# Another timetable for the last four adding transfers of a fourth weight block, in both layers of a two-layer trunk

## What is computed

```python
def squared_relu_mlp(u, w_up, w_down):
    return jnp.square(jax.nn.relu(u @ w_up)) @ w_down      # w_down: 4096 x 1024

def reference(x, mem, ...):
    ...
        h = h + rmsnorm(mixed, norm_mix_post[i])
        f = squared_relu_mlp(rmsnorm(h, norm_mlp_pre[i]), w_up[i], w_down[i])
        h = h + rmsnorm(f, norm_mlp_post[i])
```

## Time and profile before

| what | value |
|---|---|
| median of 3 runs | 1269.98 us (1269.67 to 1271.86) |
| the profiled execution | 1271.68 us |
| its span in the trace | 1269.9 us |
| TensorE busy | 1258.7 us, 99% |
| VectorE, ScalarE, GpSimd busy | 926.9, 754.0, 162.0 us |
| granted TensorE clock | 0.999 |
| HBM read and written | 225.69 and 70.04 MB |

### The profile page before, as it was taken

How to read it: one execution, slowest core, us unless ns; L and a number is a source line. 1 busy time by engine, 2 the same in 40 slices (tenths; PEclk the granted TensorE clock), 3 DMA queues, 4 the chain that set the end, 5 groups by cost and what they waited for, 6 DMA issues and landing times.

```text
span 1269.9 us, 19583 instructions
## 1 busy us (share of the span) xinstructions
PE 1258.7 (99%) x7655; PEld 1087.2 (86%) x7655; DVE 926.9 (73%) x1264; ACT 754.0 (59%) x1277; POOL 162.0 (13%) x195
## 2 busy tenths in 40 slices
PE   9999999999999999999999999999999999999998
PEld 7787878888888989999788898778889999988886
DVE  5676775989753786687797974877567776868887
ACT  6655355678653655567565753777564566665663
POOL 0046355363000000000000000000000000000000
PEclk9999999999999999999999999999999999999999
DMA  8488876352585357949876527656227378679854
GB/s 278 146 274 268 240 170 172 109 169 86 145 220 133 121 211 214 225 150 220 251 249 190 194 76 168 131 122 150 83 67 237 132 180 231 195 202 274 245 179 149
DMA packets 110387, 230.29 MB, mean 181 GB/s; under 512 B 8135, under 2 KB 18647, under 8 KB 110039
## 3 DMA queue, kind: packets, MB, share of 16 engines
q1 hardware_dynamic: 84240, 159.93, 38.1%
q0 software_dynamic: 21760, 67.11, 24.2%
q10 hardware_dynamic: 4294, 2.00, 0.8%
HBM read 225.69 MB, written 70.04 MB: 233 GB/s over the span
## 4 chain that ended last, share of the span: by engine, by line
PE 93%; DVE 2%; DMA 2%; ACT 2%; issue 1%; SPq 0%; DVEq 0%; ACTq 0%
PE G L2380 33%; PE G L2876 4%; PE G L2878 4%; PE G L2880 4%; PE X L2839 4%; PE X L2837 4%; PE X L2835 4%; PE X L2403 4%; PE X L2876 3%; PE X L2878 3%; PE X L2880 3%; PE X L2465 3%; PE G L2465 3%; PE G L2839 3%; PE G L2837 3%; PE G L2835 3%
## 5 line engine op out<-in xcount | busy, mean ns | idle before, releaser
L1380 ACT ACTIVATE whi<-raw 128x1024 fp32r<-128x1024 f32 x112 | 118.1, 1058 | 108.6 <-DMA raw<-tsum 31.1
L2132 DVE TENSOR_TENSOR wlo<-raw,whi 128x1024 fp32r<-128x1024 f32 x112 | 135.1, 1220 | 50.0 <-ACT whi L1380 49.6
L1580 DVE TENSOR_TENSOR wlo<-raw,whi 128x1024 fp32r<-128x1024 f32 x77 | 94.6, 1229 | 79.8 <-ACT whi L868 79.8
L1298 ACT ACTIVATE whi<-raw 128x1024 fp32r<-128x1024 f32 x84 | 88.8, 1060 | 103.1 <-PE X L2839 52.6
L2065 DVE TENSOR_TENSOR wlo<-raw,whi 128x1024 fp32r<-128x1024 f32 x84 | 102.7, 1222 | 58.2 <-ACT whi L1298 57.6
L2380 PE MATMUL G<-uhi,whi 128*128 128x512 f32 x352 | 144.8, 411 | 0.2 <-DVE ulo L1597 0.2
L2380 PE MATMUL G<-uhi,wlo 128*128 128x512 f32 x352 | 137.7, 391 | 0.0
L2380 PE MATMUL G<-ulo,whi 128*128 128x512 f32 x352 | 137.3, 390 | 0.0
L868 ACT ACTIVATE whi<-raw 128x1024 fp32r<-128x1024 f32 x77 | 81.4, 1058 | 77.1 <-PE G L2380 29.9
L770 POOL DMA_DIRECT2D tsum<-in_w_down x32 | 32.9, 1040 | 622.0 <-PE G L2380 328.0
L2876 PE MATMUL G<-whi,left_hi 128*128 128x512 f32 x224 | 87.4, 390 | 0.7 <-DVE wlo L2132 0.7
(11 more groups left out here) (457 smaller groups left out, 3691.2 us busy)
## 6 DMA issues: line engine op xcount, KB each, us to landing
tsum<-in_w_down POOLq DMA_DIRECT2D x48, 1024.0 KB, 10.1
raw<-in_w_up SPq DMA_DIRECT2D x64, 512.0 KB, 5.9
raw<-tsum SPq DMA_DIRECT2D x64, 512.0 KB, 4.1
raw<-in_w_down SPq DMA_DIRECT2D x48, 512.0 KB, 5.1
raw<-in_ssd_w_out SPq DMA_DIRECT2D x16, 512.0 KB, 4.3
raw<-in_swa_w_in SPq DMA_DIRECT2D x16, 512.0 KB, 4.4
csrow<-cs_rows SPq DMA_DIRECT2D x16, 384.0 KB, 4.5
raw<-in_swa_w_out SPq DMA_DIRECT2D x12, 512.0 KB, 3.9
```

Source lines behind the costliest of these rows:

```text
L1298: act.activation(whi[n % 4][:, :, :], up_right(g, r, q), ACT.Copy).then_inc(hi_done, up_fill(g, k))
L1380: act.activation(whi[n % 4][:, :, :], down_raw[n % 4][:, :, :], ACT.Copy).then_inc(hi_done, 1)
L1580: dve.tensor_tensor(wlo[q][:, :, :], src[:, :, :], whi[q][:, :, :].bitcast(F32), ALU.subtract).then_inc(lo_done, 1)
L2132: dve.tensor_tensor(wlo[n % 4][:, :, :], down_raw[n % 4][:, :, :], whi[n % 4][:, :, :].bitcast(F32), ALU.subtract).then_inc(lo_done, 1)
```

## The change

Only the two tuples are changed. Every transfer is still issued, in the same order, by the same engine. Of layer 0 the last four numbers were 117, 121, 124, 128 and become 126, 133, 150, 157, that is panels -3, 1, 4, 8 of the down phase become 6, 13, 30, 37. Of layer 1 they were 262, 268, 274, 280 and become 259, 267, 282, 289, that is panels 6, 12, 18, 24 become 3, 11, 26, 33. So the four transfers of a layer lie within 31 panels of its down phase, two ahead of the load of scale rows (panel 16) and two behind it.

```diff
 COPY_AT = (2, 4, 6)
-W0_SUM_AT = tuple(range(54, 64, 2)) + (72, 74) + tuple(range(77, 121, 4)) + (121, 124, 128)
-W1_SUM_AT = tuple(range(182, 196, 2)) + (208, 210) + tuple(range(213, 257, 4)) + (262, 268, 274, 280)
+W0_SUM_AT = tuple(range(54, 64, 2)) + (72, 74) + tuple(range(77, 117, 4)) + (126, 133, 150, 157)
+W1_SUM_AT = tuple(range(182, 196, 2)) + (208, 210) + tuple(range(213, 257, 4)) + (259, 267, 282, 289)
```

## The result

Side by side on the chip (22 runs each) the changed kernel takes 1273.06 us at the median and the kernel before 1271.13 us; the ratio is 1.0016, with a 95% interval of 1.0009 to 1.0022. So it is 2.0 us (1.1 to 2.8) slower. The forecast was no change, 1269.9 us with a range up to 1272.4; the measured time lies outside, 3.2 us above the forecast. Two things came together. The kernel before itself is 1.15 us slower here than the three runs that were shown (1269.98), and the sum had the wrong sign. One run of 2520.42 us, among the 11 of e5, is left out of its ratio; what made it so long is not known.

A forecast was written before the change was run, and what follows sets the result against it. TensorE was taken as the bound, busy 1258.7 of 1269.9 us, with 1.2 us to win. The terms -1.2 + 0.9 + 0.2 = -0.1 us gave 1269.9 us, range 1268.5 to 1272.4.

The forecast's parts named there:

- 1.2 us is all that a new timetable can win: Down phases: TensorE lost 1.2 us at panels 13 and 14 of layer 0, none in layer 1; 0.1% of the time.
- Removed, -1.2: Layer 0, panels 13 and 14: waits blamed on two overlapping adding transfers go away, -1.2 us.
- Panel 13's transfer, +0.9: Layer 0: the transfer moved to panel 13 delays panel 20's held-back load behind two scale rows; a stall of 0.9 us.
- Layer 1, panel 3, +0.2: Layer 1: the transfer moved to panel 3 delays panel 9's load; a stall between 0 and 1.2 us, taken as 0.2.
- The others cost nothing: Transfers at layer 0's panels 30 and 37 and layer 1's 11, 26 and 33 cause no stall, 0 us.
- One adding transfer in the steady part is covered: Steady down phase: a load may take 14.4 us before TensorE waits; beside an adding transfer it takes up to 12.4 us.
- s(n): Start of down-phase panel n, counted at 2.72 us a panel; the panel must have landed 2.3 us before it.
- signs of being right: No wait at layer 0's panels 13 and 14, about a microsecond at panel 20, none or little at layer 1's panel 9.
- one of being wrong: Signs against: a wait still at layer 0's panel 12 or 13, any in panels 30 to 48, or panel 20 in time.
- The slower rival: Held-back load meets the transfer: 3.1 us stall at layer 0's panel 20, 1.2 at layer 1's panel 9; 1273.1 us, chance 0.10.
- faster: Whole kernel: a gain that measurement can tell from no change, about 0.2% or 2.5 us; chance 0.03.
- M6 becomes the wait: Layer 0's last transfer holds back M6's first load by 1.7 us, with 9 us to spare; still 1269.9 us, chance 0.03.

The follow-up runs named there:

- e5: Kernel before, with both layers' four transfers at panels 10, 23, 28 and 33 of the down phase; ratio 0.9988 to the kernel before, median 1270.09 us.
- e8: The changed kernel again with no edit, for a second profile; layer 0's down phase 155.96 us, layer 1's 152.12 us.
- e1: Kernel before with the new numbers (126, 133, 150, 157) in layer 0 only, layer 1 old; ratio 1.0021 to the kernel before.
- e10: Changed kernel with layer 0's last transfer at panel 41 (161) of the down phase, not 37; layer 0's down phase 156.69 us.
- e2: Layer 0 with 126, 133, 143, 150 (a transfer at panel 23, none at panel 37), layer 1 old; ratio 0.9994 to the kernel before.
- e3: Layer 0 with 126, 132, 150, 157 (second transfer one panel sooner than in the changed kernel), layer 1 old; ratio 1.0006 to the kernel before.

## Why the prediction was wrong

**"1.2 us is all that a new timetable can win."** Wrong. It was read from one execution, and TensorE's waits in a down phase differ from one execution to the next: 1.3, 0, 0 and 0.2 us in layer 0 with the old numbers, 0 to 3.4 us in layer 1. A first step that failed was to take "in layer 1 TensorE never waited" for a property of the timetable.

**Removed, -1.2.** The waits at panels 13 and 14 did go in every execution with the new numbers. But on average they are worth less, 0.4 us (154.25 less 153.87).

**Panel 13's transfer, +0.9.** 1.1, 0.2 and 0.6 us in the three executions of these numbers, 0.6 on average. The place and roughly the size were right, the mechanism in part. I had said that panel 20's own load is late behind two scale rows. That is what e8 and e1 show. In the first profile its part is at most 0.3 us (landed 8.9 us after s(16), against a deadline of 8.6), and so the 0.9 came near the 1.1 there by luck: panel 19 was late, and VectorE's 4.6 us of fixed work behind it made panel 20 late. That path is not in the prediction.

**Layer 1, panel 3, +0.2.** 0: panel 9 had 1.8 and 1.2 us to spare. The whole of layer 1's part is a gain of 0.65 us by the means, which the sum had at +0.2.

**"The others cost nothing."** This is the failed step that decided the sign. "One adding transfer in the steady part is covered" rested on a deadline of s(n) - 2.3 us for every panel, which is the time of one copy and one subtraction. At panel 46 it is not 2.3 us from the panel that is late: side work makes panel 46 hang on the copy of panel 44, 12.0 us ahead of it. Panel 44 has therefore to land by s(46) - 12.0 = s(44) - 6.6, 4.3 us sooner than I had it. Its 14.4 us of allowance are 10.1, and the loads of panels 44 and 45, behind the transfer of panel 37, took 7.4 to 11.8 us. Measured: 0.6, 2.6 and 1.1 us at panel 46 in the three executions, 0.6 us at panel 54 in each.

Panel 54 has but 0.4 us to spare in the kernel before (low part done at 731.46, first matmul 731.89 us): with the half panels TensorE comes to it 3.5 us after panel 52 and not 5.4, so the count s(n) is 2.0 us off there, and VectorE, which has no pause from low part 46 on, brings all of panel 46's loss along.

Put together, -0.4 + 0.6 + 1.4 + 0.6 - 0.65 is +1.6 us by the means of these executions, where the prediction had -1.2 + 0.9 + 0.2. The prediction's signs of being right all came (panels 13, 14, 9 and 20, where the copy began 8.9 us after s(16) and not 9.5), and with them one of being wrong, a wait in panels 30 to 48.

**The slower rival** (held-back load, 0.10) came nearest in time, 1273.1 us against 1273.06, and by luck: it started from a kernel before that was 1.15 us too fast, and had 3.1 us at panel 20 and 1.2 at panel 9, where 0.6 and 0 were measured, and nothing at panel 46. The chance of "faster", 0.03, is also more than the 0.02 of the only case that was to give it. **M6 becomes the wait** was rightly put aside: in the changed kernel SP waited 1.5 us for the landed quarters, until 700.3, but the load could not go out before 703.3 anyhow, when its buffer came free; e10 shows what it costs four panels later. The Trainium skill, page "DMA: Bandwidth & Descriptors", section "Queues, rings and completion order", says that each DMA engine takes the queues in turn, a packet at a time. The prediction's estimate from it was a load some 3 us longer. The loads of 10.2 and 10.1 us, alone 3.5 to 4.6 us, again did not bear this estimate out; but nothing hung on it.

## What to carry to other kernels

Before you put background transfers into a stretch, make a table of spare times for every step of the pipeline, and look for its thin places. Here they came from in-order side work on the engines between load and matmul (panels 46 and 54) and from a load that is held back (panel 20), not from the transfers. In this kernel a transfer cost time where a thin place lay 5 to 9 panels behind it, or where the one before it, seven panels ahead, had not yet let the spare time come back (panel 18 in e2). And take such a table from several executions: a kernel whose engines run with 1 us to spare waits in some executions and not in others.

## What the runs showed that I had not expected

An adding transfer of 1 MB in a down phase was in flight between 10.7 and 16.0 us, and the one at panel 30 of layer 0 alone, the same bytes at the same place, took 11.4, 13.6, 14.3, 15.8 and 16.0 us in five executions (e3, the changed kernel, e8, e1, e10). Loads beside such transfers took up to 13.0 us. The instructions are the same in each execution of a kernel, and yet the runs of the kernel before lie between 1269.5 and 1276.4 us; that these landing times make all of this spread is argued from the profiles, not shown.
